# Unread TensorE products at the beginning, the attention's end and the borders, and RG-LRU's chunk 7 split before its neighbours' work

## The reference, cut to what matters

```python
for layer in range(2):                       # first block
    h = rms_norm(x, norm_mix_pre[layer])
    h = dilated_attention_mixer(h, ...) if layer == 0 else rglru_mixer(h, ...)
    x = x + rms_norm(h, norm_mix_post[layer])
    h = rms_norm(x, norm_ffn_pre[layer])
    h = conv_ffn(h, ...)                     # up, causal conv, gelu gate, down
    x = x + rms_norm(h, norm_ffn_post[layer])
for l in range(2):                           # second block
    h = _rmsnorm(x, norm_g[l])
    ...                                      # NSA, FoX and memory attention, gated, merged
    x = x + u @ w_out[l]
```

```python
h = x @ w_in                                 # 8 chunks "in", 8 chunks "gb"
xb = causal_dwconv(xb, conv_w, conv_b)
r, i = sigmoid(xb @ ga_w + ga_b), sigmoid(xb @ gx_w + gx_b)   # 4 blocks of 256 features
log_a = 8 * r * log_sigmoid(lam)
b = sqrt(max(-expm1(2 * log_a), 0)) * i * xb
hs = scan(a, b)
out = (hs * gelu(gb)) @ w_out
```

## Time and profile before

| | us |
|---|---|
| Median of 3 executions | 3152.12 |
| Fastest, slowest | 3145.02, 3157.09 |
| Profiled execution: own time | 3149.67 |
| Profiled execution: span of the trace | 3148.2 |
| TensorE matmul busy | 3038.3 |
| GpSimd busy | 1914.3 |
| DVE busy | 1479.3 |
| ScalarE busy | 803.7 |

### The profile page before, as it was taken

How to read it: one execution, slowest core, us unless ns; L and a number is a source line. 1 busy time by engine, 2 the same in 40 slices (tenths; PEclk the granted TensorE clock), 3 DMA queues, 4 the chain that set the end, 5 groups by cost and what they waited for, 6 DMA issues and landing times.

```text
span 3148.2 us, 41951 instructions
## 1 busy us (share of the span) xinstructions
PE 3038.3 (97%) x15402; PEld 2515.3 (80%) x15410; DVE 1479.3 (47%) x3183; ACT 803.7 (26%) x1757; POOL 1914.3 (61%) x2206
## 2 busy tenths in 40 slices
PE   7999999899999888999989999999999999999999
PEld 6888887688888767888878887788888887788887
DVE  2333334357740583777223646663333554665232
ACT  1111111222210342222112115552101213555100
POOL 5555554579987687899775761114777583111776
PEclk9999999899999999999999999999999999999999
DMA  4222222123222222223323220001233231000222
GB/s 148 90 88 89 87 85 89 54 74 101 94 100 95 69 78 72 95 96 99 111 83 121 94 81 28 21 28 61 95 108 113 88 100 54 28 28 22 93 98 90
DMA packets 66874, 255.71 MB, mean 81 GB/s; under 512 B 7664, under 2 KB 8176, under 8 KB 64880
## 3 DMA queue, kind: packets, MB, share of 16 engines
q1 hardware_dynamic: 62496, 227.57, 21.8%
q10 hardware_dynamic: 4176, 25.47, 2.2%
HBM read 250.91 MB, written 2.10 MB: 80 GB/s over the span
## 4 chain that ended last, share of the span: by engine, by line
PE 90%; DVE 4%; ACT 2%; issue 2%; POOL 1%; DMA 0%; ACTq 0%; DVEq 0%; POOLq 0%
PE bank L360 23%; PE bank L362 23%; PE bank L361 22%; PE bank L1762 3%; PE bank L1736 2%; PE bank L1747 2%; PE bank L398 2%; PE bank L388 2%; PE bank L622 1%; PE bank L390 1%; PE bank L389 1%; PE bank L1731 1%; POOL w_lo L2086 1%; PE bank L1233 1%; PE bank L1490 1%
## 5 line engine op out<-in xcount | busy, mean ns | idle before, releaser
L2086 POOL TENSOR_TENSOR w_lo<-w_raw,w_hi 128x256 fp32r<-128x256 f32 x1736 | 1383.0, 827 | 36.2
L2082 POOL TENSOR_SCALAR w_hi<-w_raw 128x1024 fp32r<-128x1024 f32 x434 | 486.1, 1120 | 1159.2 <-PE bank L362 1040.6
L360 PE MATMUL bank<-in_hi,w_hi 128*128 128x512 f32 x1408 | 555.0, 394 | 2.9 <-ACT factor_wide L451 2.1
L362 PE MATMUL bank<-in_hi,w_lo 128*128 128x512 f32 x1408 | 549.2, 390 | 0.0
L361 PE MATMUL bank<-in_lo,w_hi 128*128 128x512 f32 x1408 | 548.8, 390 | 0.0
L360 PE MATMUL bank<-z_hi,w_hi 128*128 128x512 f32 x976 | 394.6, 404 | 1.4 <-ACT z_factor_wide L451 1.4
L362 PE MATMUL bank<-z_hi,w_lo 128*128 128x512 f32 x976 | 383.2, 393 | 0.0
L361 PE MATMUL bank<-z_lo,w_hi 128*128 128x512 f32 x976 | 382.5, 392 | 0.0
L360 PEld LDWEIGHTS bank<-in_hi,w_hi 128*128 128x128 f32 x1408 | 264.9, 188 | 56.7 <-ACT factor_wide L451 2.8
L362 PEld LDWEIGHTS bank<-in_hi,w_lo 128*128 128x128 f32 x1408 | 264.7, 188 | 55.7
L361 PEld LDWEIGHTS bank<-in_lo,w_hi 128*128 128x128 f32 x1408 | 264.9, 188 | 53.1
(11 more groups left out here) (418 smaller groups left out, 5032.4 us busy)
## 6 DMA issues: line engine op xcount, KB each, us to landing
w_raw<-in_units SPq DMA_DIRECT2D x434, 512.0 KB, 3.4
bias<-in_bias ACTq DMA_DIRECT2D x8, 1152.0 KB, 5.1
o_all<-in_cmp_w ACTq DMA_DIRECT2D x4, 2048.0 KB, 8.3
x_res<-in_x ACTq DMA_DIRECT2D x4, 512.0 KB, 8.9
mem_in<-in_mem ACTq DMA_DIRECT2D x2, 1024.0 KB, 6.0
out<-x_res ACTq DMA_DIRECT2D x4, 512.0 KB, 2.6
consts<-in_consts ACTq DMA_DIRECT2D x1, 710.5 KB, 3.8
both_layers_cols<-in_layer_cols ACTq DMA_DIRECT2D x2, 140.5 KB, 4.7
```

The costliest lines, as they stand in the source:

```text
L360: pe.matmul(out, hi[:, w], rh, start=start and n == 0, stop=False)
L362: last = pe.matmul(out, lo[:, w], rh, start=False, stop=stop and n == len(tiles) - 1)
L2082: d = c.s.unit_hi.on(pool.tensor_scalar(c.w_hi[s][:, :], c.w_raw[s][:, :], 1.0, 0.0, ALU.mult, ALU.add))
L2086: last = pool.tensor_tensor(c.w_lo[s][:, w], c.w_raw[s][:, w], c.w_hi[s][:, w].bitcast(F32), ALU.subtract)
```

## The change

A new function issues a number of f32 products of ones by ones with 128 columns each, into a bank that nobody reads before it is written anew. It is called with 40 products as soon as ones is written; with 6 and 16 around the last pieces of the attention; and at each of the four borders with 6, 10 and 16: ahead of the wait for the squares, after the sums, and after the transposes. That is 190 products in all. In RG-LRU the split of chunk 7 moves on ScalarE ahead of gates 2, and on DVE ahead of roots 2 and 3.

```diff
--- before.py
+++ after.py
@@ -428,12 +428,22 @@
     pe.wait_ge(*c.s.wide_ready[z.name])
 
 
+def pe_warm(pe, c, b, times):
+
+    for _ in range(times):
+        pe.matmul(c.bank[b][:, 0:P], c.ones[:, :], c.ones[:, :], start=True, stop=True)
+
+
 def pe_post_begin(pe, c, name):
+    b = 4 if name == "attn_out" else 2
+    pe_warm(pe, c, b, 6)
     pe.wait_ge(*c.s.squares_added[name, DC - 1])
     pe.wait_ge(*c.s.bank_copied[name, DC - 1])
     pe_sum_tokens(pe, c, c.bank[7], c.acc, TT, True, True, ("post", name))
+    pe_warm(pe, c, b, 10)
     pe.wait_ge(*c.s.factor_found["post", name])
     pe_spread(pe, c, c.bank[6], c.narrow, TT, ("post", name))
+    pe_warm(pe, c, b, 16)
 
 
 
@@ -666,8 +676,10 @@
             pe_logits_one(pe, c, a, r + 1)
             next(pieces)
         pe_values_one(pe, c, a, r)
+    pe_warm(pe, c, 4, 6)
     for _ in pieces:
         pass
+    pe_warm(pe, c, 4, 16)
 
 
 def act_turned_out_one(act, c, a, r):
@@ -1004,8 +1016,8 @@
             act_lru_gates(act, c, n // 2 - 2)
             act_lru_decay(act, c, n - 4)
             act_lru_decay(act, c, n - 3)
+    act_lru_parts(act, c, DC - 1)
     act_lru_gates(act, c, 2)
-    act_lru_parts(act, c, DC - 1)
     act_lru_decay(act, c, 4)
     act_lru_decay(act, c, 5)
     act_lru_gates(act, c, 3)
@@ -1088,9 +1100,9 @@
         if n == 5:
             dve_lru_root(dve, c, 0)
             dve_lru_root(dve, c, 1)
+    dve_lru_parts(dve, c, DC - 1)
     dve_lru_root(dve, c, 2)
     dve_lru_root(dve, c, 3)
-    dve_lru_parts(dve, c, DC - 1)
     dve_lru_root(dve, c, 4)
     dve_lru_root(dve, c, 5)
     dve_lru_gb(dve, c, z, 0)
@@ -2019,6 +2031,7 @@
 def pe_program(pe, c):
     norms = c.norms()
     pe.wait_ge(*c.s.ones_set["all"])
+    pe_warm(pe, c, 4, 40)
     pe.wait_ge(*c.s.ident_loaded["all"])
     pe_attention_one(pe, c, norms["attn"])
     pe_out(pe, c, "attn_out", [("attn_out", n) for n in range(DC)], c.oh, c.ol, (0, 1, 2, 3), begun=3)
```

## The result

The changed kernel took 3123.56 us, median of 4 runs (3122.61 to 3127.12), beside 3153.75 for the kernel before on the same chip, median of 4 (3145.02 to 3157.09): a ratio of 0.9911, 95% interval [0.9888, 0.9933]. The forecast was 3122 in 3109 to 3138. Run once more, later, it had a median of 3126.22 (5 runs, 3125.54 to 3130.82) and a ratio of 0.9945 [0.9925, 0.9964]; the nine runs together have a median of 3126.0. The kernel before was run 75 times in all: median 3152.5, standard deviation 5.2, range 3140.0 to 3157.3. In words: 26 to 30 us faster, 0.9%. The times also scatter less: the nine of the changed kernel lie within 8.2 us, those 75 within 17.3.

A forecast was written before the change was run, and what follows sets the result against it. TensorE, busy for 97% of the span, was taken as the bound, losing time to waits and its low clock level. Gains 3.5 + 2.7 + 16.1 + 5.5 = 27.8 us took 3149.7 to 3122 us, range 3109 to 3138.

The forecast's parts named there:

- Products at 0.22 us, each block ending 0.3 to 0.5 us before its wait: Added blocks: each product costs 0.22 us (ends 0.21 and 0.43), so border blocks finish 0.3 to 0.5 us early.
- both rivals in which the products don't bring or hold the level at the borders: Four borders: level lost all the same, 3138.0 us, 13%; or products cost 0.43 and overrun, 3169.6 us, 5%.
- The bound for an overrun: Four borders: worst case -18.6 us if the blocks outlast their waits (4.3 - 2.55 and 6.9 - 3.96, four times).
- The start, 3.5: Kernel start: forty products before ident lands let the first two k steps run at full level, gaining 3.5 us.
- the rival that the clock is lost: Kernel start: TensorE idles 0.5 to 3 us after the fortieth product and loses the level; 3125.4 us, 7%.
- The attention's end, 2.7: Attention's end: six and sixteen products fit in waits, and thirteen product starts leave the low level, gaining 2.7 us.
- The borders, 16.1: Four borders: 14.0 us of k-step excess goes and lo comes 0.52 us sooner at each, gaining 16.1 us.
- RG-LRU, 5.5: RG-LRU's last chunk: earlier split of chunk 7 ends gates 3 6.7 us sooner; 1.2 lost on GpSimd, gaining 5.5.
- The rival that GpSimd keeps its place: RG-LRU's output units: GpSimd's saturated stretch doesn't move, so the RG-LRU edit is worth nothing; 3127.4 us, 13%.
- The allowance of 1.2 for GpSimd: RG-LRU: GpSimd's first unit and DVE's chain lose 1.2 us, with DVE's roots now beside that unit.
- Nothing else changes: Rest of the kernel, including the second block: no change, 0 us in the sum.
- The excesses as draws of one thing: Four borders: the level's return varies by execution, so another run of the kernel before loses 6.0 to 30.2 us.

The follow-up runs named there:

- run 75: Not a label but a count: the kernel before, unchanged, was run 75 times in all; median 3152.5 us, range 3140.0 to 3157.3.
- e7_double: The changed kernel with 12, 20 and 32 products at the four borders in place of 6, 10 and 16: 3147.25 us, ratio 0.9985 to the kernel before.
- e5_without_16: The changed kernel without the sixteen products behind the transposes at the four borders: 3147.05 us, ratio 0.9987 to the kernel before.
- e10_pair: The changed kernel with 48 products at the start and 22 more ahead of RG-LRU's second output unit: 3121.21 us, ratio 0.9920 to the kernel before.
- e4_dve_half: The changed kernel with ScalarE's order of before in RG-LRU, VectorE's as changed: 3123.06 us, ratio 0.9917 to the kernel before.
- e1_lru_only: The kernel before with RG-LRU's chunk 7 split sooner on both engines and no added products: 3154.01 us, ratio 0.9998.
- e9_lru_again: The kernel before with RG-LRU's chunk 7 split sooner and no added products, profiled and timed once more: 3147.77 us, ratio 0.9994.

## Why the prediction was right, step by step

- **Products at 0.22 us, each block ending 0.3 to 0.5 us before its wait.** Right: 0.22 and 0.23 (e7_double), and waits of 0.46, 0.21 and 0.41 are left at the first border. So both rivals in which the products don't bring or hold the level at the borders fell. The bound for an overrun was added up slightly wrong: 4.3 - 2.55 and 6.9 - 3.96, four times, are 18.8 and not 18.6, and the first block of six would have overrun as well.
- **The start, 3.5.** 3.6 in the profiled execution, and that is partly luck: the rival that the clock is lost had 7% and is what half of the eight profiles show, at a cost of 1.6 to 3.5 us of the first stretch. Its premise (a gap of 0.5 to 3 us, by when the level rises) was right, and its chance too small. By the prediction's own terms forty products end between 12.3 and 13.6, not between 11.5 and 14; they ended at 11.6 to 13.2, since the level rose sooner than it allowed for in four of eight. The kernel before varies here too: its first vt transpose was at 43.72 and 42.01, so the second profile would have left a gain of 1.9.
- **The attention's end, 2.7.** 2.65 measured.
- **The borders, 16.1.** Measured 15.7: 14.0 of excess as predicted, and lo 0.44 sooner instead of 0.52, four times. That the excess goes is shown: all six profiles with blocks of 6, 10 and 16 products have 18.2 us from k0 to unit 3 at every border. That it was 14.0 to the tenth is so because the prediction read it off the execution that it is compared with; four profiles of kernels without products have 14.0, 11.8, 13.9 and 21.7. e5_without_16 shows it from the other side: without the last block 17.5 us of excess are back.
- **RG-LRU, 5.5.** 6.1 in its stretch. The rival that GpSimd keeps its place fell: the pair's second unit came 5.9 us nearer to gates 2. The allowance of 1.2 for GpSimd was too large in this profile: its wait at the pair grew by 0.5, and in the other profiles with the new order, e10_pair left aside, it was between 4.44 and 5.08, against 4.56 and 4.57 with the old one. The delay of ScalarE's gates 2 was there (the last one ends at 1097.8, gates 3 starts at 1097.92) and cost nothing, and the edit on ScalarE brings nothing (e4_dve_half).
- **Nothing else changes.** This step, which stood in the sum as a zero, failed, though small: the second block took 3.0 us more for the same instructions. What the low level cost in it rose from 10.6 to 14.0 us. In the changed kernel's second profile the block took 1486.5, so a part of the 3.0 varies from run to run.
- **The excesses as draws of one thing.** The prediction leant here on the Trainium skill (TensorE: Matmul & The Clock Gate, Part 1), by which the cycle runs freely, so that another execution of the kernel before would have other excesses at its borders. The runs bear it out in part. Two profiles of the kernel before had excesses of 14.0 and 11.8 us between k0 and unit 3 over the four borders (18.2 each being full), within 0.2 of each other at three of the four. But two profiles of the RG-LRU order alone had 13.9 and 21.7, and differed by 1.9, 3.7 and 5.9 us at three of the four, as that rule of the Trainium skill has it. Over the 75 runs of the kernel before the time has a standard deviation of 5.2. On the other side, border 4 and the second block repeated within 0.2 us in both kernels, and differed between the kernels: e1_lru_only and e9_lru_again.

**Where 5.6 us can vanish.** In the kernel before, the RG-LRU order saves 5.6 us where it stands, and 0.6 with an uncertainty of 2.5 in the time. Both profiles of it show 6.3 us more at border 4 and in the second block, for the same instructions at a lower level. That would account for the loss, but it isn't shown to be the cause of it: borders 1 to 3, which have no part in this sum, moved by 7.7 between the two profiles. In the changed kernel the borders can no longer take part, since they are full in every profile, and the same edit is worth 6 to 9 us of time. That a saving upstream shifts the waits that follow, and with them where the level falls and returns, is a reading that no run here tests; what fixes the length of the low stretches was not found. All eleven profiles of kernels with VectorE's new order, products or not, have 1486.5 to 1494.3 us in the second block, all three without it 1483.4 to 1485.2; the changed kernel's two differ by 1.7, more than the 1.3 between the groups.

## What to carry to other kernels

Where TensorE is the bound and waits some us at a border for a chain of other engines, the wait costs twice, as idle time and as low clock behind it; unread products or transposes that end just before the wait does take away the second cost, and what overruns the wait is paid in full. Fill the last wait before dense work first, and let the fill reach up to it: at the start gaps up to 1.7 us went with a kept level here and those from 2.1 with a lost one, though a shorter block went with the latter too. Judge a saving of a few us by its stretch and by the time together, with a second profile of either kernel: low stretches elsewhere can differ by as much as the saving, and between two executions of one kernel by more.

## What the runs showed of the hardware

- Transposes held the level as well as products: 18.2 us from k0 to unit 3 at all four borders.
- The level can come back inside a block of sixteen 128-column products (4.5 to 5.8 us instead of 3.5) and is there for the k steps behind it.
- Low stretches of the second block repeated between two executions to the hundredth of the granted clock in a window, for the kernel before (1.00, 0.96) and for that with the RG-LRU order alone (0.83, 0.87). They didn't for the changed kernel (0.91 and 0.87, then 1.00 and 0.91), nor did borders 1 to 3 of the RG-LRU order alone (65.3 and 73.1 us from k0 to unit 3).
- At the start the granted clock is no witness. The window of the kernel before from 14.33 to the level's return, in the columns of the windows above, has it at 1.00, while its products are spaced for the low level:

```profile
14.33:22.40 8.07, 8.07 (x28) 6.91 (x29) 0.75 (x1) 1.24 (x2) 3.08 (x5) 1.00 0.65 255
```
